# The last four activation tiles of two down projections begin some bytes further on

## What is computed

```python
# first block, hidden width 5632
x = x + (jax.nn.silu(h @ ffn_w_gate[l]) * (h @ ffn_w_up[l])) @ ffn_w_down[l]

# second block, hidden width 5632, conv over three tokens
up = h @ w_up
y = conv_b + conv_w[0] * padded[:, 0:seq]
for tap in range(1, CONV_WIDTH):
    y = y + conv_w[tap] * padded[:, tap:tap + seq]
gate, val = jnp.split(y, 2, axis=-1)
return (jax.nn.silu(gate) * val) @ w_down
```

## Time and profile before

| | before |
|---|---|
| three runs, median (lowest to highest) | 2509.73 us (2506.45 to 2510.35) |
| the profiled execution, its own time | 2507.64 us |
| its span, first to last instruction | 2505.9 us |
| granted TensorE clock, mean | 0.992 |
| TensorE busy with matmuls | 2439.3 us, 97% of the span |
| VectorE, ScalarE busy | 1484.8 us (59%), 1122.4 us (45%) |

### The profile page before, as it was taken

The page is one execution under the profiler, slowest core; times in us unless marked ns, Lnnn a source line. Parts: engine busy times, 40 slices in busy tenths (PEclk is TensorE's granted clock), DMA queues, the critical chain, the costliest instruction groups (busy, mean ns, idle before and its releaser), DMA issues.

```text
span 2505.9 us, 57361 instructions
## 1 busy us (share of the span) xinstructions
PE 2439.3 (97%) x24650; PEld 2411.0 (96%) x24650; DVE 1484.8 (59%) x1683; ACT 1122.4 (45%) x1061; POOL 114.1 (5%) x93
## 2 busy tenths in 40 slices
PE   7999978989999999999999999999999999999998
PEld 7999968889999999999999999989999999999998
DVE  6557597665555555554444567674576666665444
ACT  4334424354444444443344443454455555544332
POOL 3000050000200000000020200000200000000000
PEclk9999989999999999999999999999999999999999
DMA  7455400116555555556665565625555555555554
GB/s 232 166 187 196 135 6 4 37 69 193 188 190 197 188 195 190 193 192 192 194 192 194 169 237 200 218 86 191 187 194 191 194 189 196 187 197 188 200 187 148
DMA packets 171387, 431.72 MB, mean 172 GB/s; under 512 B 17614, under 2 KB 23387, under 8 KB 170107
## 3 DMA queue, kind: packets, MB, share of 16 engines
q1 hardware_dynamic: 170027, 422.30, 50.0%
q10 hardware_dynamic: 1232, 7.52, 0.8%
HBM read 427.59 MB, written 2.17 MB: 171 GB/s over the span
## 4 chain that ended last, share of the span: by engine, by line
PE 91%; DVE 7%; ACT 2%; issue 1%; DMA 0%; DVEq 0%; SPq 0%; ACTq 0%
PE ps L1947 28%; PE ps L1948 28%; PE ps L1949 28%; DVE LOW L1073 1%; ACT HIW L606 1%; PE ps L2101 1%; DVE TM L1346 0%; ACT H_ROWS L648 0%; DVE LO L1350 0%; DVE TT L1347 0%; DVE CV L1380 0%; DVE GT L1362 0%; PE ps L2139 0%; DVE TMP L1293 0%; PE ps L2045 0%
## 5 line engine op out<-in xcount | busy, mean ns | idle before, releaser
L1073 DVE TENSOR_TENSOR LOW<-RAW,HIW 128x2048 fp32r<-128x2048 f32 (+1 forms) x397 | 911.9, 2297 | 921.9 <-ACT HIW L606 921.8
L1947 PE MATMUL ps<-H_ROWS,HIW 128*128 128x256 f32 x4928 | 1367.3, 277 | 20.1 <-DVE LOW L1073 17.5
L1948 PE MATMUL ps<-H_ROWS,HIW 128*128 128x256 f32 x4928 | 1366.1, 277 | 0.0
L1949 PE MATMUL ps<-H_ROWS,LOW 128*128 128x256 f32 x4928 | 1364.9, 277 | 0.0
L606 ACT ACTIVATE HIW<-RAW 128x2048 fp32r<-128x2048 f32 (+1 forms) x397 | 760.8, 1917 | 1196.4 <-PE ps L1949 1192.5
L1947 PEld LDWEIGHTS ps<-H_ROWS,HIW 128*128 128x128 f32 x4928 | 928.4, 188 | 22.1 <-DVE LOW L1073 18.5
L1949 PEld LDWEIGHTS ps<-H_ROWS,LOW 128*128 128x128 f32 x4928 | 928.9, 188 | 0.0
L1948 PEld LDWEIGHTS ps<-H_ROWS,HIW 128*128 128x128 f32 x4928 | 928.1, 188 | 0.1
L1947 PE MATMUL ps<-HID,HIW 128*128 (+1 forms) x1408 | 388.7, 276 | 0.0
L1948 PE MATMUL ps<-HID,HIW 128*128 (+1 forms) x1408 | 388.6, 276 | 0.0
L1949 PE MATMUL ps<-HID,LOW 128*128 (+1 forms) x1408 | 388.6, 276 | 0.0
(11 more groups left out here) (365 smaller groups left out, 1515.3 us busy)
## 6 DMA issues: line engine op xcount, KB each, us to landing
RAW<-in_ffn_w_up SPq DMA_DIRECT2D x264, 512.0 KB, 4.3
RAW<-in_ffn_w_down SPq DMA_DIRECT2D x176, 512.0 KB, 4.5
RAW<-in_fox_w_in SPq DMA_DIRECT2D x98, 512.0 KB, 4.4
RAW<-in_w_in SPq DMA_DIRECT2D x96, 512.0 KB, 4.1
RAW<-in_ffn_w_gate SPq DMA_DIRECT2D x88, 512.0 KB, 3.7
RAW<-in_w_out SPq DMA_DIRECT2D x32, 512.0 KB, 5.0
RAW<-in_fox_w_out SPq DMA_DIRECT2D x32, 512.0 KB, 4.8
INV<-rows_out ACTq DMA_DIRECT2D x4, 1024.0 KB, 7.5
```

What stands on the lines that cost most here:

```text
L1073: V.tensor_tensor(LOW[:, u_const % 4, 0:n], RAW[:, u_const % 4, 0:n], HIW[:, u_const % 2, 0:n].bitcast(F32), ALU.subtract).then_inc(lo_mad ...
L1947: mm(o_, hi_w, h_hi, start=start, stop=False)
L1948: mm(o_, hi_w, h_lo, start=False, stop=False)
L1949: i = mm(o_, lo_w, h_hi, start=False, stop=stop)
```

## The change

`HID` becomes a function over `HID_ROWS`, whose rows are 80 floats (320 bytes) longer. Tiles 0 to 39 keep their places in the row. Tiles 40 to 43 begin 8, 16, 24 and 32 floats (32, 64, 96 and 128 bytes) further on in the first down phase, and 40, 48, 56 and 64 floats (160, 192, 224 and 256 bytes) further on in the second. Since a row is longer, every tile of the low row lies 320 bytes further on as well, and all that lies at `f0` 640 bytes.

```diff
-        HID = at("HID", [P, 2, FT, T], r2, F32R)
-        f0 = r2 + 2 * FT * T * 4
+        HID_ROWS = at("HID_ROWS", [P, 2, FT * T + 80], r2, F32R)
+
+        def HID(part, k0, n=1, second=False):
+
+            row = HID_ROWS[:, part, :]
+            if not isinstance(k0, int) or k0 < FT - 4:
+                return row[:, 0:FT * T].rearrange("p (k t) -> p k t", t=T)[:, bass.ds(k0, n), :]
+            c = (FT - 4) * T + 8 + 32 * second
+            return row[:, c:c + 4 * (T + 8) - 8 + 8].rearrange("p (k t) -> p k t", t=T + 8)[:, k0 - (FT - 4):k0 - (FT - 4) + n, 0:T]
+        f0 = r2 + 2 * (FT * T + 80) * 4
...
-                    A(HID[:, 0, bass.ds(g * 4, 4), :], HS[:], ACT.Copy).then_inc(S("hid_hi"), 1)
+                    A(HID(0, g * 4, 4), HS[:], ACT.Copy).then_inc(S("hid_hi"), 1)
...
-            def down(u0, n0, made0):
+            def down(u0, n0, made0, second=False):
...
                     for j in range(18, 22):
                         unit(b + j, [2 * j, 2 * j + 1], GROUP, plain, last=j == 21,
-                             hcol=lambda part, k: HID[:, part, k, :], h_wait=(S("hid_made"), made0 + 11))
+                             hcol=lambda part, k: HID(part, k, 1, second)[:, 0, :], h_wait=(S("hid_made"), made0 + 11))
...
-            down(U_DOWN2, N_DOWN2, 12)
+            down(U_DOWN2, N_DOWN2, 12, second=True)
```

More of the change, by code:

```diff
@@ L1049, in tail_ffn2 @@
                     act.wait_ge(S("hid_full"), g + 12)
-                    A(HID[:, 0, bass.ds(g * 4, 4), :], YV[:], ACT.Copy).then_inc(S("hid_hi"), 1)
+                    A(HID(0, g * 4, 4, True), YV[:], ACT.Copy).then_inc(S("hid_hi"), 1)
             ffn_phase(U_FFN2, tail_ffn2, 3)
@@ L1724, in tail_ffn1 @@
                     dve.wait_ge(S("hid_hi"), g + 1)
-                    V.tensor_tensor(HID[:, 1, bass.ds(g * 4, 4), :], HS[:],
-                                    HID[:, 0, bass.ds(g * 4, 4), :].bitcast(F32), ALU.subtract)\
+                    V.tensor_tensor(HID(1, g * 4, 4), HS[:],
+                                    HID(0, g * 4, 4).bitcast(F32), ALU.subtract)\
                         .then_inc(S("hid_made"), 1)
@@ L1898, in tail_ffn2 @@
                     dve.wait_ge(S("hid_hi"), g + 12)
-                    V.tensor_tensor(HID[:, 1, bass.ds(g * 4, 4), :], YV[:],
-                                    HID[:, 0, bass.ds(g * 4, 4), :].bitcast(F32), ALU.subtract)\
+                    V.tensor_tensor(HID(1, g * 4, 4, True), YV[:],
+                                    HID(0, g * 4, 4, True).bitcast(F32), ALU.subtract)\
                         .then_inc(S("hid_made"), 1)
@@ L1986, in down @@
                         unit(b + j, [2 * j, 2 * j + 1], GROUP, plain, j == 0, n0=n0 + 8 * half,
-                             hcol=lambda part, k: HID[:, part, k, :], h_wait=(S("hid_made"), made0 + 10))
+                             hcol=lambda part, k: HID(part, k, 1, second)[:, 0, :], h_wait=(S("hid_made"), made0 + 10))
                     with pe.Fori(0, 4) as i:
@@ L1990, in down @@
                             unit(b + 2 + j, [4 + 2 * j, 5 + 2 * j], GROUP, plain, g=i, step=4,
-                                 hcol=lambda part, k: HID[:, part, bass.ds(i * 8 + k, 1), :])
+                                 hcol=lambda part, k: HID(part, i * 8 + k)[:, 0, :])
                     for j in range(18, 22):
                         unit(b + j, [2 * j, 2 * j + 1], GROUP, plain, last=j == 21,
-                             hcol=lambda part, k: HID[:, part, k, :], h_wait=(S("hid_made"), made0 + 11))
+                             hcol=lambda part, k: HID(part, k, 1, second)[:, 0, :], h_wait=(S("hid_made"), made0 + 11))
             pe.sem_inc(unit_used, FREE_UNITS)
```

## The result

| | before | changed |
|---|---|---|
| median (lowest to highest), four runs each | 2509.17 us (2506.45 to 2510.35) | 2534.44 us (2532.59 to 2535.86) |
| the profiled execution, its own time | 2507.64 us | 2535.48 us |
| its span | 2505.9 us | 2533.7 us |

The ratio is 1.0100 with a 95% interval of 1.0087 to 1.0112: the change makes the kernel 25 us, 1%, slower. I had forecast 2512.1 us and a range up to 2520.0.

A forecast was written before the change was run, and what follows sets the result against it. The prediction took TensorE's matmul pace to bound the kernel. To the median of 2509.73 us it added 2.4 for moved tiles and 0 for the low row, writers and buffers: 2512.1 us, range 2505.5 to 2520.0.

The forecast's parts named there:

- What bounds the kernel: In the down phases TensorE waits for nobody; a phase lasts as long as its matmuls take, about 113.3 ns each.
- The moved tiles: Tiles 40 to 43 in the down phases: 16 visits at 0.15 us each, 2.4 us; paying this had chance 0.40.
- My bound of 1.2 us: Moved tiles, between the bounds: only those not beginning at a multiple of 64 bytes pay, which is half.
- The low row: Low row 320 bytes further on for all tiles in the down phases: taken to cost 0.
- the rule of 64 bytes: Guess that a tile beginning at a multiple of 64 bytes costs nothing; 320, five times 64, would then be free.
- The bound of that step: Upper bound for the low row's shift: 1280 matmuls reading it in tiles 0 to 39, 6.4 ns each, 8.1 us.
- The low rows pay as well: Rival: every down-phase matmul reading the low row slows, 10.5 us with the moved tiles, 2520.2 us; chance 0.12.
- A slower pace that stays: Rival: moved tiles leave each down phase's second half at 4.5 ns more a matmul, 9.5 us, 2521.6 us; chance 0.05.
- A better pace: Rival: the low row's new distance removes a pace loss, 2504.7 us or less; 0.08 together with a slower pace ended.

The follow-up runs named there:

- moved_512: Changed kernel with rows 128 floats longer instead of 80, so the low row lies 512 bytes further on; 2511.94 us against 2509.68 before.
- both_16: Kernel before with both hidden-activation rows 16 bytes further on, the low row another 256, no tile moved within a row; 2534.21 us against 2510.27.
- low_320: Kernel before with only the low row of the hidden activations 320 bytes further on, no tile moved within its row; 2534.37 us against 2509.68.
- low_64: Kernel before with only the low row of the hidden activations 64 bytes further on, no tile moved within its row; 2535.18 us against 2509.68.
- weights_64: Kernel before with both weight buffers and both hidden-activation rows 64 bytes further on, normalised stream left in place; 2581.85 us in one run.
- low_256: Kernel before with only the low row of the hidden activations 256 bytes further on, no tile moved within its row; 2516.08 us against 2517.92.
- last_64: Kernel before with tile 15 of the normalised stream moved by 256 bytes in place of 240; 2505.14 us against 2517.92.
- last_0: Kernel before with tile 15 of the normalised stream not moved at all; 2504.17 us against 2517.92.
- hid_240: Changed kernel with tiles 40 to 43 all moved by 240 bytes and the low row 256 bytes further on; 2513.04 us against 2510.27 before.
- best_240: hid_240 with the normalised stream's last tile moved by 256 bytes; median 2511.79 us against 2510.27 before, ratio 1.0038.

## Why the prediction was wrong

**What bounds the kernel** was right: TensorE waits for nobody in the down phases, before or after, and only the pace of a matmul moved the time.

**The moved tiles** were priced right by the visit. I took 0.15 us from tile 15 of the normalised stream and had 2.4 us in sum. moved_512 shows 0.12 to 0.14 us for each of 14 visits, 1.8 us, and two that are free. That its medians are 2.3 us above before, so near to 2.4, is in part luck: the profiled execution reaches 3.2 with 1.4 us of the slower pace, which the sum didn't have. In the changed kernel the term doesn't come on top of the low row's: its moved tiles pass at 117.5 to 118.8 ns, no slower than tiles 0 to 39 at 119.2. My bound of 1.2 us, by multiples of 64 bytes, was wrong in its rule: 64 and 192 bytes cost as much as 32 or 160, and of the eight displacements only 256 is seen to be free. The 16-byte lines of the Trainium skill (SBUF — State Buffer, section Specifications), by which no displacement would cost anything, don't describe this either: 16 bytes is one whole line, and both_16 loses 24 us.

**The low row** is the step that failed. "320 is five times 64, so under the rule of 64 bytes it costs nothing ... I take 0." The rule of 64 bytes was one of three guesses for what makes tile 15 slow, and I let it decide where I had no row. low_320 and low_64 show 5.9 ns for each of 2112 matmuls and 12.5 us a phase. The two distances at which the old kernel runs at 113.3 ns differ by an odd multiple of 512 bytes, which is a multiple of 256 as well; they were compatible with every power of two up to 512 bytes as the period and no evidence for 64.

**The bound of that step** was too low too. I gave it 8.1 us, the price on the matmuls that read the low row. The trace of the changed kernel has all three lines above 276 ns, at 283, 281 and 281, and the price falls on all 4224 matmuls: 25 us. That the two matmuls beside the one that reads the low row pay as well is shown (low_320 has 121.1, 118.9 and 117.8 ns between starts); by what coupling is not.

**The rivals.** "The low rows pay as well" was the right mechanism with a chance of 0.12, at 8.1 us for the low row where low_320 shows 25. "A slower pace that stays" was right in kind: it follows the moved tiles in the changed kernel. There it saves a little, since 117.8 ns is less than 119.2, and tiles with the low row 64 bytes off pass in that pace as fast as tiles at the old place do. The changed kernel's phases are 0.6 and 1.6 us shorter than those of low_320. "A better pace" wasn't seen in any of the 13 kernels: none has matmuls of 256 columns in these products at less than 113.3 ns.

## What to carry to other kernels

When an address changes, ask what else the new layout moves: here padding a row for four tiles shifted the other forty. A float32r product that loads a weight block for each 256 columns has a step that depends on where the moving tiles lie against the weight blocks, so pad rows and buffers of such operands by multiples of 256 bytes, all against the same reference. 256 and 512 bytes were free here; of ten displacements between multiples of 256 one was seen to be (176), by no rule that these runs show. And a rule guessed from one row must not set another term to zero; the lower and the upper bound then have to carry that term for all neighbours in the pipeline.

## What the runs showed of the hardware

- The step of a float32r matmul of 128 x 256 with its own weight load was 113.3 ns where tile and weight blocks lay as before (64 bytes apart within 256), and 117.5 to 120.0 ns at the other places tried, at a granted clock of 1.00. The exception is 176 bytes off, in tile 15 of weights_64: 113.3 ns behind its first matmuls, in all 38 groups. The step was 119.2 ns with one of the two rows off by 64 bytes, 120.0 ns with both, and 118.4 ns over a group with the weight blocks off by 64 the other way.
- The Trainium skill, in SBUF — State Buffer, section A bandwidth-pool intuition that's wrong, gives TensorE a second, independent read port for its weight loads. In weights_64 the pace depends on both places all the same: moving the weight blocks alone made the normalised stream 5 ns a matmul slower, and moving blocks and tiles together gave the old pace back to 0.01 us in 239. Where the two meet, no run here shows.
- There is a second pace at the best place, 117.8 ns, with a record of 281 ns in place of 276. It is entered behind some short waits and not behind others: the same break in the second down phase left it in low_256 and weights_64, and left 113.3 ns in the profiled executions of before, moved_512, last_64, last_0, hid_240 and best_240. It lasts over hundreds of matmuls. What decides it stays open.
- Tiles 240 bytes off were followed by 113.3 ns wherever tiles at the old place came behind them without a wait. In moved_512 tiles 128 bytes off, behind others 32 to 96 bytes off, were followed by 117.8 ns both times in the first down phase. That the 128 bytes do it, and not the tiles before, isn't shown.
